# A second attention that forms keys and values per head, multiplies values in pairs of 64 columns, and divides by sums spread through memory

## The chip, the cores and the metric

The kernel runs on one core of one Trainium2 chip, in one launch. The metric is the device time of one execution in microseconds; the time given is the median of several runs. PE is TensorE, DVE is VectorE, ACT is ScalarE, POOL is GpSimd and SP is SyncE, whose queue issues nearly all DMAs. All matmuls of the part that is changed are fp32, and each fp32 matmul shows as two matmul instructions in the profile (a transpose shows as one).

## The reference

Two blocks follow one another on a 1024 x 1024 activation. The first (two layers of latent attention, Fourier mixing and gated merging) isn't touched. The second block projects x, selects keys by an indexer, and runs the attention in which the change lies; an S5 branch, a GLU, an output projection and a layer norm complete it. What the change computes otherwise:

```python
q_lat = einsum('bshd,hcd->bshc', qh, w_uk) * ATT_HEAD_DIM ** -0.5    # 8 heads, d = 64, latent c = 128
_, sel = lax.top_k(index_score, n_sel)                               # 256 of the causal keys per query
s = einsum('bthc,btkc->bthk', q_lat, c_sel)                          # scores against the shared latent
p = softmax(where(valid, s, neg))
o_lat = einsum('bthk,btkc->bthc', p, c_sel)                          # latent output, 128 wide
att = einsum('bshc,hcd->bshd', o_lat, w_uv)                          # back to 64 per head
y = concat([att * silu(gate_a), ssm * silu(gate_s)]) @ w_out         # then layer_norm(ALPHA * x + y)
```

Since the latent c is shared by the heads, `q_lat . c` equals `q . (w_uk c)`, a key of 64 per head, and `(p c) w_uv` equals `p (c w_uv)`, a value of 64 per head. Both orders compute the same function.

## The kernel before

A list of instructions is written out by hand for each engine; semaphores tie them. The eight PSUM banks (128 x 512 fp32 each) have a "full" semaphore that the producer raises and a "free" one that the reader raises; `begin(b)` waits for free, `arrive(b)` for full.

**Ahead of the attention.** DVE picks the top keys by rounds of MAX8 and MATCH_REPLACE8 (L2012, L2013) over `sel`; for the last query tile 16 of the 32 rounds are left over (the list `LATE`) and done inside the attention, one in each of heads 1, 3, 5, 6, 7 of tiles 4 to 6 and in head 7 of tile 3. PE meanwhile computes gates and, last, the queries qT2 (`gates(5, 0)`, L735). Then it turns w_uk (L892) and forms `qlT`, all 8 heads' latent queries, in 16 matmuls of 64 rows and 512 columns (L903), which ACT copies out of PSUM with the scale (L1490). When they are done SP loads the layer-norm gain and bias (L1149, L1150), each spread over 128 partitions, and DVE waits for these and for the GLU (L2046, L2047) before the first unit.

**The attention.** A unit u is one of 8 query tiles t (128 queries) and one of 8 heads h, with the heads inner. Tile t sees t + 1 key tiles. For each unit: PE scores against `c2T` (L918, one or two matmuls of up to 512 columns over 128 rows), into banks 0/1 or 2/3 in turn. DVE adds the mask, takes the maximum and writes to `Pb2` (L2110). ACT exponentiates and sums the row (L1519). PE turns the t + 1 key tiles of the probabilities (L930), DVE copies the first four from PSUM (L2095, `turned`), ACT the rest (L1513). PE issues the scores of unit u + 1 before it turns unit u, so one unit is ahead.

Per tile, four heads' turned probabilities are side by side, and `latent_out` (L940) multiplies each key tile of `c2` by all four at once, 512 columns wide: one call at head 5, one at head 1 of the next tile. ACT copies the result (L1495), `att_out` (L948) multiplies each head's 128 x 128 latent by w_uv, DVE scales by the inverted sums (L2051, L2053), `att_turn` (L956) turns the tile back, and DVE multiplies it into the gate (L2060). `out_half` (L969) is half of an output product, 4 fp32 matmuls of 512 columns; four of them run at heads 4 to 7 for the tile before. DVE adds the residual x (`residual`, L2069), takes the mean (L2076) and centres it (L2078); ACT squares and takes the root (`ln_std`, L1500, L1501; the root's table and the exponential's are loaded in turn); DVE finishes the norm (`layer_norm`, L1842, L2087), and SP writes the tile out and reloads the next x tile (L1090).

The first attention (L535 to L575) already multiplies values as the change will: `v_tok` in pairs of 64 columns, two units side by side in the array.

## Time and profile before

| | us |
|---|---|
| median of 3 runs | 2722.01 (2720.97 to 2722.5) |
| the profiled execution, its own time | 2720.86 |
| its span in the trace | 2719.1 |
| busy: PE / DVE / ACT | 2574.2 / 1364.7 / 796.1 |
| mean granted clock of TensorE | 0.976 |
| first unit of the second attention starts at | 2398.85 |

Times in the trace count from the start of the span. A busy time is the union of an engine's instructions; a matmul's own duration is longer than its distance from the next, because they are pipelined. So "start to start" is what a matmul costs in a row of them, and the chain (which cuts each piece where the next begins) shows it directly.

### The profile page before, as it was taken

The numbers are of one execution on the slowest core, as the hardware profiler recorded it, in microseconds if no ns is written. First come the engines' busy times: TensorE is split into PE (matmuls) and PEld (weight loads), VectorE is DVE, ScalarE is ACT, GpSimd is POOL, SyncE is SP. The second block draws the span as 40 slices with busy tenths as digits, with TensorE's granted clock in tenths as the row PEclk, the third lists the DMA queues.
The fourth block names the chain that finished last, engine by engine and source line by source line (L and its number), as shares of the span: only waits on it lengthen the run. The fifth ranks groups of instructions, "written<-read, shape, count | busy, mean of one in ns | idle before, by whom it ended". The sixth has DMA issues, their size and how long they took to land.

```text
span 2719.1 us, 30167 instructions
## 1 busy us (share of the span) xinstructions
PE 2574.2 (95%) x12253; PEld 1785.7 (66%) x12253; DVE 1364.7 (50%) x2194; ACT 796.1 (29%) x1420; POOL 348.1 (13%) x463
## 2 busy tenths in 40 slices
PE   7998999899999999989979999999989989989997
PEld 6855887776666887578868766667547444445553
DVE  2353777321113243357762211122689999955763
ACT  3332445221112142334451111131352113143341
POOL 0012230000000000133200000000043863100000
PEclk9998999999999999989989999999999999999998
DMA  5010000301113121000002111130301011010000
GB/s 194 28 62 1 1 1 1 88 24 47 47 47 123 34 94 58 31 1 1 1 32 55 47 47 41 33 121 15 118 32 39 2 41 39 31 62 31 31 16 31
DMA packets 106378, 118.89 MB, mean 44 GB/s; under 512 B 20704, under 2 KB 76736, under 8 KB 106240
## 3 DMA queue, kind: packets, MB, share of 16 engines
q1 hardware_dynamic: 105088, 112.76, 13.3%
q10 hardware_dynamic: 1152, 4.19, 0.4%
q8 instruction: 98, 1.61, 0.2%
q14 instruction: 40, 0.33, 0.0%
HBM read 98.92 MB, written 16.84 MB: 43 GB/s over the span
## 4 chain that ended last, share of the span: by engine, by line
PE 84%; DVE 8%; ACT 4%; issue 1%; POOL 1%; SPq 1%; DMA 1%; DVEq 0%; POOLq 0%; ACTq 0%
PE PS L644 8%; PE PS L614 6%; PE PS L617 6%; PE PS L620 6%; PE PS L551 6%; PE PS L441 4%; PE PS L575 4%; PE PS L561 4%; PE PS L969 4%; PE PS L735 4%; PE PS L882 2%; PE PS L658 2%; PE PS L661 2%; PE PS L664 2%; PE PS L940 2%; PE PS L486 2%
## 5 line engine op out<-in xcount | busy, mean ns | idle before, releaser
L614 PE MATMUL PS<-hHi,R2bR 128*128 128x512 f32 x768 | 306.3, 399 | 15.4 <-ACT rows L1323 15.4
L617 PE MATMUL PS<-hLo,R2bR 128*128 128x512 f32 x768 | 300.2, 391 | 0.0
L620 PE MATMUL PS<-hHi,R2bR 128*128 128x512 f32 x768 | 300.0, 391 | 0.0
L1737 DVE TENSOR_TENSOR R2bR<-W,R2bR 128x1024 fp32r<-128x1024 f32 x48 | 57.5, 1222 | 309.6 <-ACT R2bR L1311 309.6
L1343 ACT ACTIVATE R3a<-PS,pT 128x512 f32<-128x512 f32 x64 | 42.3, 687 | 467.5 <-PE PS L620 467.5
L614 PEld LDWEIGHTS PS<-hHi,R2bR 128*128 128x128 f32 x768 | 145.1, 189 | 48.8 <-ACT rows L1323 15.7
L1712 DVE TENSOR_REDUCE negm<-PS 128x1 f32<-128x1024 f32 x128 | 156.5, 1223 | 28.3 <-PE PS L551 23.4
L735 PE MATMUL PS<-hT,W 128*128 128x512 f32 x384 | 166.8, 595 | 0.0
L617 PEld LDWEIGHTS PS<-hLo,R2bR 128*128 128x128 f32 x768 | 145.1, 189 | 33.0 <-issue 3.3
L1295 ACT ACTIVATE R2b<-PS,negm 128x1024 f32<-128x1024 f32 x128 | 142.4, 1112 | 78.6 <-DVE negm L1712 78.6
L620 PEld LDWEIGHTS PS<-hHi,R2bR 128*128 128x128 f32 x768 | 145.0, 189 | 30.4
L2165 POOL TENSOR_TENSOR R<-R,rsh 128x768 f32<-128x768 f32 x16 | 23.8, 1486 | 1028.0 <-DVE rsh L1669 831.8
L561 PE MATMUL PS<-ident,R2b 128*128 128x128 f32 x1024 | 139.0, 279 | 7.3 <-ACT R2b L1295 5.6
L2012 DVE MAX8 ssc<-R2a 128x8 f32<-128x384 f32 (+4 forms) x160 | 132.4, 828 | 5.4
L575 PE MATMUL PS<-R2b,R 128*64 128x128 f32 x2048 | 128.3, 279 | 6.5 <-DVE R2b L1725 3.2
L735 PEld LDWEIGHTS PS<-hT,W 128*128 128x128 f32 x384 | 73.0, 191 | 91.1 <-issue 91.0
L575 PEld LDWEIGHTS PS<-R2b,R 128*64 128x64 f32 x2048 | 112.7, 139 | 29.1 <-issue 22.3
L2013 DVE MATCH_REPLACE8 R2a<-ssc,R2a 128x384 f32<-128x384 f32 (+4 forms) x160 | 129.4, 809 | 0.0
L561 PEld LDWEIGHTS PS<-ident,R2b 128*128 128x128 f32 x1024 | 114.3, 142 | 22.5 <-issue 13.2
L1772 DVE TENSOR_TENSOR R3a<-R3a,PS 128x512 f32<-128x512 f32 x64 | 43.8, 685 | 162.4 <-PE PS L644 162.3
L441 PE MATMUL PS<-W,hT 128*128 128x256 f32 (+1 forms) x512 | 122.3, 399 | 0.7 <-DMA W<-in_w_in 0.5
L969 PE MATMUL PS<-W,R 128*128 128x512 f32 x256 | 117.2, 603 | 0.8 <-DVE R L2060 0.8
(347 smaller groups left out, 4758.5 us busy)
## 6 DMA issues: line engine op xcount, KB each, us to landing
W<-in_w_in SPq DMA_DIRECT2D x10, 2048.0 KB, 8.2
W<-in_w_in SPq DMA_DIRECT2D x33, 512.0 KB, 4.9
xres<-R SPq DMA_DIRECT2D x3, 4096.0 KB, 18.8
W<-in_w_out SPq DMA_DIRECT2D x6, 2048.0 KB, 8.0
R<-xres SPq DMA_DIRECT2D x2, 4096.0 KB, 18.3
W<-in_c_dft_s SPq DMA_DIRECT2D x2, 2052.0 KB, 9.2
R<-in_x ACTq DMA_DIRECT2D x8, 512.0 KB, 7.9
W<-in_w_in SPq DMA_DIRECT2D x4, 1024.0 KB, 6.8
```

Of the source, the lines that this page charges most:

```text
L441: mm = pe.matmul(o[:, 0:hi - lo], hT[:, k, t * P:(t + 1) * P], wc[:, k, lo:hi], start=(k == 0), stop=(k == 7))
L551: mm = pe.matmul(PS[:, b + n, :], x[0:QK, t * P:(t + 1) * P], y[0:QK, n * 512:(n + 1) * 512], start=(i == 0), stop=(i == 2))
L561: mm = pe.transpose(o[:, k * P:(k + 1) * P], Pb[u % 2][:, c * P:(c + 1) * P], ident[:, :])
L575: mm = pe.matmul(PS[e * VD:(e + 1) * VD, 6, at_], v_tok[:, k, h, :], PT[e][:, k * P:(k + 1) * P], start=(k == 0), stop=(k == 7))
L614: mm = pe.matmul(o, wHi[c % 2][:, k, :], hHi[:, k, ns], start=(k == 0), stop=False)
L617: mm = pe.matmul(o, wHi[c % 2][:, k, :], hLo[:, k, ns], start=False, stop=False)
L620: mm = pe.matmul(o, wLo[c % 2][:, k, :], hHi[:, k, ns], start=False, stop=(k == 7))
L644: mm = pe.matmul(o, g[:, k0 + k, :], rhs[:, k, n * 512:(n + 1) * 512], start=(k == 0), stop=(k == 3))
L735: mm = pe.matmul(o, wz[:, k, m * P:(m + 1) * P], xT[:, k, n * 512:(n + 1) * 512], start=(k == 0), stop=(k == 7))
L969: mm = pe.matmul(o, mix[:, k, t * P:(t + 1) * P], wo[:, k, :], start=(k == 0), stop=(k == 7))
L1295: act.activation(Pb[u % 2], PS[:, b:b + 2, :].rearrange("p a c -> p (a c)"), ACT.Exp, bias=negm[:, u:u + 1], accum_out=rsum[:, u:u + 1]).t ...
L1712: dve.tensor_reduce(negm[:, u:u + 1], PS[:, b:b + 2, :].rearrange("p a c -> p (a c)"), AX.X, ALU.max, negate=True).then_inc(s_nm, 1)
```

## The change

`qlT`, `wukT`, `latent_out`, `att_out` and `att_turn` go. Keys per head `kT2` (8 matmuls of c2T by w_uk, 512 columns) and values `v2` (8 matmuls) are formed before the attention. Scores take 64 rows, in the upper or lower half of the array by the head's parity. `pv_pair2` multiplies a pair of heads at a time, each key tile by two 64-column matmuls of 128 columns, right into the transposed layout. The inverted sums no longer scale rows there: SP writes them to memory and reads them back spread over 64 partitions per head, and `att_gate` multiplies by them. `lng`, `lnb` move to the buffer of the block's transposed input. The output halves move: n = 1 at heads 5 and 7 of the next tile, n = 0 at heads 1 and 3 of the one after; layer norm and root move to heads 7 and 6.

```diff
-        wukT = CT.rearrange("p i q c -> p (i q c)").rearrange("p (m c) -> p m c", m=4)
-        wuv = Bb.rearrange("p i q c -> p (i q c)").rearrange("p (h d) -> p h d", h=H)
-        qlT = R0
+        wuv = Bb.rearrange("p i q c -> p (i q c)")
+        kT2 = r0[:, 0:4096].rearrange("p (m s) -> p m s", m=4)
+        v2 = r0[:, 4096:8192].rearrange("p (t c) -> p t c", t=NT)
         xt = [r3b[:, 2048:3072], r3b[:, 3072:4096]]
-        lng, lnb = r3a[:, 0:1024], r3a[:, 1024:2048]
-        att = [r3a[:, 2048:2560], r3a[:, 2560:3072]]
-        olT = [r3a[:, 3072:3584], r3a[:, 3584:4096]]
-        PT2 = [hTf[:, i * 4096:(i + 1) * 4096].rearrange("p (k c) -> p k c", k=NT) for i in range(2)]
+        PT2 = [hTf[:, i * 1024:(i + 1) * 1024] for i in range(4)]
+        lng, lnb = hTf[:, 4096:5120], hTf[:, 5120:6144]
+        att = hTf[:, 6144:6656].rearrange("p (m c) -> p m c", m=4)
+        rbc = [hTf[:, 7168 + 512 * i:7680 + 512 * i].rearrange("p (m c) -> p m c", m=4) for i in range(2)]
+        rsums2 = nc.dram_tensor("rsums2", (NT, 2, H // 2, P), F32, kind="Internal").ap()
...
-            qT_free = [bk.count(b) for b in range(8)]
             pe.wait_ge(s2_wk, 16)
-            o = begin(0)
             for m in range(4):
-                mm = pe.transpose(o[:, m * P:(m + 1) * P], wuk[:, m * P:(m + 1) * P], ident[:, :])
-                if m == 0:
-                    mm.then_inc(w_used[1], 1)
-            mm.then_inc(full[0], 1)
-            for b in range(8):
-                pe.wait_ge(free[b], qT_free[b] + (b == 0))
-            for h in range(H):
                 for n in range(2):
-                    b = (1 + 2 * h + n) % 8
+                    b = 2 * m + n
                     o = begin(b)
-                    r_ = slice(VD * (h % 2), VD * (h % 2) + VD)
-                    pe.matmul(o, wukT[r_, h // 2, :], qT2[r_, h // 2, n * 512:(n + 1) * 512],
+                    pe.matmul(o, wuk[:, m * P:(m + 1) * P], c2T[:, n * 512:(n + 1) * 512],
                               start=True, stop=True).then_inc(full[b], 1)
-            marks["qlat"] = bk.count(0)
+            pe.nop().then_inc(w_used[1], 1)
+            pe.wait_ge(s2_wv, 16)
+            for t in range(NT):
+                o = begin(t)
+                pe.matmul(o, c2T[:, t * P:(t + 1) * P], wuv, start=True, stop=True).then_inc(full[t], 1)
             marks["attention"] = list(bk.n)
 
...
-            pe.wait_ge(s2_wv, 16)
 
+                r_ = slice(VD * (h % 2), VD * (h % 2) + VD)
                 for n in range((w + 511) // 512):
-                    mm = pe.matmul(PS[:, b + n, 0:min(512, w - 512 * n)], qlT[:, h, t * P:(t + 1) * P],
-                                   c2T[:, n * 512:min(w, n * 512 + 512)], start=True, stop=True)
+                    mm = pe.matmul(PS[:, b + n, 0:min(512, w - 512 * n)], qT2[r_, h // 2, t * P:(t + 1) * P],
+                                   kT2[r_, h // 2, n * 512:min(w, n * 512 + 512)], start=True, stop=True)
...
-            def latent_out(t, hg):
-                u = H * t + 4 * hg + 3
-                pe.wait_ge(free[4], pt2[u][0])
-                pe.wait_ge(free[5], pt2[u][1])
-                o = begin(6)
+            def pv_pair2(p):
+
+                t, m = p // 4, p % 4
+                pe.wait_ge(free[4], pt2[2 * p + 1][0])
+                pe.wait_ge(free[5], pt2[2 * p + 1][1])
+                if m == 0:
+                    begin(6)
                 for k in range(t + 1):
-                    mm = pe.matmul(o, c2[:, k, :], PT2[hg][:, k, :], start=(k == 0), stop=(k == t))
-                mm.then_inc(full[6], 1)
-                ol_free[hg] = bk.count(6)
-
-            def att_out(t):
-                o = begin(7)
-                pe.wait_ge(free[6], ol_free[1])
-                for h in range(H):
...
-            def att_turn(t):
-                pe.wait_ge(free[7], bk.count(7))
-                o = begin(6)
-                for k in range(4):
-                    mm = pe.transpose(o[:, k * P:(k + 1) * P], att[t % 2][:, k * P:(k + 1) * P], ident[:, :])
-                mm.then_inc(full[6], 1)
-                turn_free[0] = bk.count(6)
...
-            def out_half(t, n, half):
+                    for e in range(2):
+                        h = 2 * m + e
+                        mm = pe.matmul(PS[VD * e:VD * e + VD, 6, m * P:(m + 1) * P], v2[:, k, h * VD:(h + 1) * VD],
+                                       PT2[(2 * p + e) % 4][:, k * P:(k + 1) * P], start=(k == 0), stop=(k == t))
+                if m == 3:
+                    mm.then_inc(full[6], 1)
+
+            def out_half(t, n, half, b=7):
 
                 if (n, half) == (1, 0):
-                    pe.wait_ge(free[6], turn_free[0])
+                    pe.wait_ge(s2_gate, t + 1)
-                o = begin(6 + n) if half == 0 else PS[:, 6 + n, :]
+                o = begin(b) if half == 0 else PS[:, b, :]
-                    mm.then_inc(full[6 + n], 1)
-
-            pt2, ol_free, turn_free = {}, {}, {}
+                    mm.then_inc(full[b], 1)
...
                     scores2(u + 1)
-
-                if h == 5:
-                    latent_out(t, 0)
-                if t >= 1:
-                    if h == 1:
-                        latent_out(t - 1, 1)
-                    if h == 2:
-                        att_out(t - 1)
-                    if h == 3:
-                        att_turn(t - 1)
-                    if h >= 4:
-                        out_half(t - 1, 1 - (h - 4) // 2, h % 2)
+                if u >= 2 and u % 2 == 0:
+                    pv_pair2(u // 2 - 1)
+                if h in (1, 3) and t >= 2:
+                    out_half(t - 2, 0, h // 2)
+                if h in (5, 7) and t >= 1:
+                    out_half(t - 1, 1, h // 2 - 2)
                 p_turn2(u)
-            latent_out(NT - 1, 1)
-            att_out(NT - 1)
-            att_turn(NT - 1)
-            for i in range(4):
-                out_half(NT - 1, 1 - i // 2, i % 2)
+            pv_pair2(4 * NT - 1)
+            for half in range(2):
+                out_half(NT - 2, 0, half)
+            for half in range(2):
+                out_half(NT - 1, 1, half, 4)
+            for half in range(2):
+                out_half(NT - 1, 0, half, 5)
 
 
...
-            sp.wait_ge(full[0], marks["qlat"])
+            for b in range(8):
+                sp.wait_ge(full[b], marks["attention"][b])
             small(lng, a["ln_g_2"][0].partition_broadcast(P), s2_ln)
             small(lnb, a["ln_b_2"][0].partition_broadcast(P), s2_ln)
             sp.wait_ge(s_xsave, 16 * (L + 1))
+            for t in range(2):
+                small(xt[t], xres[t * P:(t + 1) * P, :], s2_xt[t])
             for t in range(NT):
-                if t >= 2:
-                    sp.wait_ge(s2_od[t % 2], 16 * (t // 2))
-                small(xt[t % 2], xres[t * P:(t + 1) * P, :], s2_xt[t % 2])
+                sp.wait_ge(s2_ri, t + 1)
+                for e in range(2):
+                    sp.dma_start(rsums2[t, e].rearrange("m q -> q m"), rinv[:, H * t + e:H * t + H:2],
+                                 allow_slow_non_contiguous=True).then_inc(s2_rw, 16)
+                sp.wait_ge(s2_rw, 32 * (t + 1))
+                for e in range(2):
+                    small(rbc[t % 2][VD * e:VD * e + VD].rearrange("p m c -> p (m c)"),
+                          rsums2[t, e].rearrange("m q -> (m q)").partition_broadcast(VD), s2_bc)
                 if t >= 1:
                     sp.wait_ge(s2_o, t)
                     small(out[0, (t - 1) * P:t * P, :], xt[(t - 1) % 2], s2_od[(t - 1) % 2])
+                    if t + 1 < NT:
+                        sp.wait_ge(s2_od[(t + 1) % 2], 16 * ((t + 1) // 2))
+                        small(xt[(t + 1) % 2], xres[(t + 1) * P:(t + 2) * P, :], s2_xt[(t + 1) % 2])
...
-            o = arrive(0)
-            act.activation(wukT[:, :, :], o.rearrange("p (m c) -> p m c", m=4), ACT.Copy).then_inc(free[0], 1)
-            for h in range(H):
-                for n in range(2):
-                    b = (1 + 2 * h + n) % 8
-                    o = arrive(b)
-                    act.activation(qlT[:, h, n * 512:(n + 1) * 512], o, ACT.Copy, scale=64.0 ** -0.5
-                                   ).then_inc(free[b], 1)
-
-            def latent_copy(hg):
-                o = arrive(6)
-                act.activation(olT[hg], o, ACT.Copy).then_inc(free[6], 1)
+            for b in range(8):
+                o = arrive(b)
+                act.activation(kT2[:, b // 2, (b % 2) * 512:(b % 2 + 1) * 512], o, ACT.Copy, scale=64.0 ** -0.5
+                               ).then_inc(free[b], 1)
+            for t in range(0, NT, 2):
+                o = arrive(t)
+                act.activation(v2[:, t, :], o, ACT.Copy).then_inc(free[t], 1)
...
-                if t >= 2 and h == 2:
+                if u >= 1:
+                    turned_high(u - 1)
+                if t >= 2 and h == 6:
                     ln_std(t - 2)
...
             bk.n = list(marks["attention"])
+            for t in range(1, NT, 2):
+                dve.wait_ge(full[t], bk.n[t])
+                dve.tensor_copy(v2[:, t, :], PS[:, t, :]).then_inc(free[t], 1)
             dve.wait_ge(s2_glu, 8)
             dve.wait_ge(s2_ln, 32)
 
-            def att_norm(t):
+            def sums_inverted(t):
                 dve.wait_ge(free[2], sums2[t])
-                st.link(dve.reciprocal(rinv[:, H * t:H * t + H], rsum[:, H * t:H * t + H]))
-                o = arrive(7)
-                dve.tensor_tensor(att[t % 2].rearrange("p (h d) -> p h d", h=H), o.rearrange("p (h d) -> p h d", h=H),
-                                  rinv[:, H * t:H * t + H].unsqueeze(2).broadcast_to([P, H, VD]), ALU.mult
-                                  ).then_inc(free[7], 1)
+                dve.reciprocal(rinv[:, H * t:H * t + H], rsum[:, H * t:H * t + H]).then_inc(s2_ri, 1)
 
             def att_gate(t):
                 o = arrive(6)
+                dve.wait_ge(s2_bc, 32 * (t + 1))
+                dve.tensor_tensor(att, o.rearrange("p (m c) -> p m c", m=4), rbc[t % 2], ALU.mult).then_inc(free[6], 1)
+                dve.wait_ge(free[6], bk.count(6))
                 m = mix[:, 0:4, t * P:(t + 1) * P]
-                dve.tensor_tensor(m, m, o.rearrange("p (k c) -> p k c", k=4), ALU.mult).then_inc(free[6], 1)
-
-            def residual(t, n):
+                dve.tensor_tensor(m, m, att, ALU.mult).then_inc(s2_gate, 1)
+
+            def residual(t, n, b=7):
 
                 x = xt[t % 2]
                 if n == 1:
...
                 if n == 1:
+                    half_free[t] = (b, bk.count(b))
...
                     turned(u - 1)
+                if t >= 1:
+                    if h == 0:
+                        sums_inverted(t - 1)
+                    if h == 2:
+                        att_gate(t - 1)
-                if h == 5:
-                    bk.take(6)
                 if t >= 2:
                     if h == 0:
+                        residual(t - 2, 1)
+                    if h == 4:
                         residual(t - 2, 0)
-                    if h == 4:
+                    if h == 7:
                         layer_norm(t - 2)
-                if t >= 1:
-                    if h == 1:
-                        bk.take(6)
-                    if h == 2:
-                        att_norm(t - 1)
-                    if h == 3:
-                        att_gate(t - 1)
-                    if h == 6:
-                        residual(t - 1, 1)
             turned(H * NT - 1)
+            sums_inverted(NT - 1)
+            residual(NT - 2, 1)
             residual(NT - 2, 0)
-            bk.take(6)
-            att_norm(NT - 1)
             att_gate(NT - 1)
             layer_norm(NT - 2)
-            residual(NT - 1, 1)
-            residual(NT - 1, 0)
+            residual(NT - 1, 1, 4)
+            residual(NT - 1, 0, 5)
             layer_norm(NT - 1)
```

## Rows read from the trace of the kernel before

**Rows 1.** The page, part 1: busy time of each engine over the whole execution.
```profile
PE 2574.2 (95%) x12253; PEld 1785.7 (66%) x12253; DVE 1364.7 (50%) x2194; ACT 796.1 (29%) x1420; POOL 348.1 (13%) x463
```

**Rows 2.** Busy time by stretch: us, PE, PEld, DVE, ACT, POOL, PEclk, DMA share, GB/s.
```profile
2500.00:2600.00 100.00, 94.89 (x372) 53.99 (x371) 76.63 (x122) 39.24 (x77) 0.00 (x0) 1.00 0.06 22
```

**Rows 3.** Chain in order of time, late tile: start, us, engine, line, count.
```profile
2657.06 6.87 PE PS L940 x16
2663.92 3.43 PE PS L969 x8
```

**Rows 4.** Timeline: value products, then turns, first attention (start, us).
```profile
325.45 1.97 PE L575 MATMUL PS<-R2b,R 128*64 128x128 f32 x32
327.34 1.09 PE L561 MATMUL PS<-ident,R2b 128*128 128x128 f32 x8
```

**Rows 5.** Timeline, late tile and tail of the second attention.
```profile
2642.20 1.89 PE L948 MATMUL PS<-rt,R3a 128*128 128x64 f32 x16
2643.93 1.05 PE L930 MATMUL PS<-ident,R3b 128*128 128x128 f32 x8
...
2677.53 1.04 PE L930 MATMUL PS<-ident,R3b 128*128 128x128 f32 x8
2692.13 16.52 PE L969 MATMUL PS<-W,R 128*128 128x512 f32 x32 [0.78 <-DVE R L2060]
...
2708.69 0.69 DVE L2069 SCALAR_TENSOR_TENSOR R3b<-R3b,PS 128x512 f32<-128x512 f32 x1 [6.11 <-PE PS L969]
2711.72 1.06 ACT L1500 ACTIVATE R2b<-R3b 128x1024 f32<-128x1024 f32 x1 [21.74 <-DVE R3b L2078]
```

**Rows 6.** Timeline from before the attention to its first unit.
```profile
2384.32 0.60 PE L892 MATMUL PS<-ident,R3b 128*128 128x128 f32 x4
2385.66 7.24 PE L903 MATMUL PS<-R3a,u_mid 64*128 64x512 f32 x32 [0.74 <-ACT u_mid L1485]
2393.31 0.43 SPq L1090 DMA_DIRECT2D R3a<-in_ln_b  x1
2395.27 1.21 DVE L2013 MATCH_REPLACE8 R2b<-ssc,R2b 128x1024 f32<-128x1024 f32 x1
2398.85 0.29 DVE L2110 CUSTOM_DVE_ANT_0 R3b<-PS,R2a 128x128 f32<-128x128 f32 x1 [2.38 <-DMA R3a<-in_ln_b]
```

**Rows 7.** Timeline, first VectorE pass of tiles 1, 2, 4 and 7 (queries).
```profile
2407.90 0.42 DVE L2110 CUSTOM_DVE_ANT_0 R3b<-PS,R2a 128x256 f32<-128x256 f32 x1
2430.42 0.56 DVE L2110 CUSTOM_DVE_ANT_0 R3b<-PS,R2a 128x384 f32<-128x384 f32 x1 [0.22 <-PE PS L918]
2497.86 0.82 DVE L2110 CUSTOM_DVE_ANT_0 R3b<-PS,R2a 128x640 f32<-128x640 f32 x1
2626.95 1.22 DVE L2110 CUSTOM_DVE_ANT_0 R3b<-PS,R2b 128x1024 f32<-128x1024 f32 x1
```

**Rows 8.** Timeline around the 64-row matmuls of an earlier stage (L799).
```profile
2150.40 0.39 PE L799 MATMUL PS<-rtp,R3b 64*128 64x128 f32 x4
2150.72 1.12 PE L735 MATMUL PS<-hT,W 128*128 128x512 f32 x2
...
2254.92 0.49 PE L799 MATMUL PS<-R2b,R3b 64*128 64x128 f32 x4
2255.24 0.39 PE L799 MATMUL PS<-R2a,R3b 64*128 64x128 f32 x4
```

**Rows 9.** DMA issues: out<-in, count, KB each, median us to landing.
```profile
W<-in_w_in SPq DMA_DIRECT2D x1, 32.0 KB, 4.9
rsums<-rows SPq DMA_DIRECT2D x2, 32.0 KB, 1.8
R3a<-rsums SPq DMA_DIRECT2D x16, 256.0 KB, 5.6
```

**Rows 10.** One group from 2398 us on: busy us, mean ns | idle before, releaser.
```profile
L930 PE MATMUL PS<-ident,R3b 128*128 128x128 f32 x288 | 43.9, 279 | 15.0 <-ACT R3b L1519 14.7
```

**Rows 11.** TensorE alone by stretch: us, PE busy, granted clock, DMA share, GB/s.
```profile
2398.00:2403.00 5.00, 3.13 (x12) 0.50 0.44 176
```

More of the change, by code:

```diff
@@ L361, in build @@
         s2_xt = [sem(f"x_tile_loaded{i}") for i in range(2)]
+        s2_ri = sem("second_sums_inverted")
+        s2_rw = sem("second_sums_written")
+        s2_bc = sem("second_sums_spread")
+        s2_gate = sem("attention_gated")
         s2_r = sem("centred_ready")
@@ L1143, in _ @@
             small(wuk.rearrange("p (h d) -> p h d", h=H), a["w_uk_2"][0].rearrange("h c d -> c h d"), s2_wk)
-            small(wuv, a["w_uv_2"][0].rearrange("h c d -> c h d"), s2_wv)
+            small(wuv.rearrange("p (h d) -> p h d", h=H), a["w_uv_2"][0].rearrange("h c d -> c h d"), s2_wv)
             for n in range(2):
@@ L1502, in ln_std, with turned_high @@
                                ).then_inc(s2_sq, 1)
+            bk.n = list(marks["attention"])
+            def turned_high(u):
+                t = u // H
+                if t < 4:
+                    return
+                o = arrive(5)
+                w = (t - 3) * P
+                act.activation(PT2[u % 4][:, 512:512 + w], o[:, 0:w], ACT.Copy).then_inc(free[5], 1)
             for u in range(H * NT):
                 t, h = u // H, u % H
-                if u >= 1:
-                    tp = (u - 1) // H
-                    hp = (u - 1) % H
-                    bk.take(4)
-                    if tp >= 4:
-                        o = arrive(5)
-                        n = tp - 3
-                        act.activation(PT2[hp // 4][:, 4:4 + n, (hp % 4) * P:(hp % 4 + 1) * P],
-                                       o[:, 0:n * P].rearrange("p (k c) -> p k c", k=n), ACT.Copy).then_inc(free[5], 1)
                 b = 2 * (u % 2)
-                bk.take(b)
                 act.wait_ge(s2_nm, u + 1)
@@ L2089, in turned @@
             def turned(u):
-                t, h = u // H, u % H
-                n = min(4, t + 1)
+                t = u // H
+                w = min(4, t + 1) * P
                 o = arrive(4)
@@ L2106, in _ @@
                 if u >= 2:
-                    bp = 2 * (u % 2)
-                    dve.wait_ge(full[4 + (((u - 2) // H) >= 4)], bk.count(4 + (((u - 2) // H) >= 4)))
+                    bp = 4 + ((u - 2) // H >= 4)
+                    dve.wait_ge(full[bp], bk.count(bp))
                 dve.tensor_tensor_reduce(Pb2[u % 2][:, 0:w], PS[:, b:b + 2, :].rearrange("p a c -> p (a c)")[:, 0:w],
```

34 lines of the change are left out of this document (7 added, 27 removed).

## The prediction

> **What bounds the kernel now.** The page first: PE is busy 95% of the execution, DVE 50% [rows 1]. That is a mean over stages, so the stretch of the change is read next, in windows. From 2500 to 2600 us PE is busy 94.9 of 100 us and DVE 76.6 [rows 2]: PE bounds the attention, and DVE stands close behind it where the left-over selection rounds lie. Last, the chain of waits: in a late tile it runs through scores, the latent product (16, 6.87 us) and an output half (8, 3.43 us), PE after PE, 0.43 us per instruction of 512 columns [rows 3]. So PE instructions taken out of tiles 1 to 7 come off the time, until another engine or a latency takes over. I take as the loop the stretch from the first pass of tile 1, 2407.90 us [rows 7], to the end of the last turn, about 2678.4 [rows 5]: 270.5 us.
>
> **Removed from PE in the loop.** latent_out has 36 key tiles, two groups of heads and two instructions each, 144 in all; 2 lie in tile 0 and 16 behind the last turn, so 126 x 0.43 = 54.2 us. att_out is 16 instructions in 1.73 us (2642.20 to 2643.93) [rows 5], 7 times in the loop: 12.1. att_turn is 4 transposes at 0.11, the pace of turns by their row (8 in 1.04 us, the last one's length included) [rows 5]: 7 x 0.45 = 3.2. Of the output halves 26 instead of 28 run in the loop: 6.9 us move to the tail. Sum 76.4 us.
>
> **Added to PE in the loop.** Value pairs: the first attention does 8 key tiles of a pair, 32 instructions, in 1.89 us start to start [rows 4], 0.236 per key tile; that is about half of what the same columns cost one after the other (4 x 128 columns at 0.43 / 4), so the two column halves do run together. There are 144 such steps, 3 in tile 0's share and 8 in the tail: 133 x 0.236 = 31.4 us. Scores keep their columns, and 64 rows cost what 128 do: L903, of 64 rows, shows 32 instructions in 7.24 us only because neighbouring ones lie in opposite halves [rows 6]; here the two matmuls of a unit lie in the same half and nothing stands beside them, so 0.43 each stays. No gain there.
>
> **Changes of shape in the array.** New in each unit: from 128-row turns to 64-row scores, and on to something else. In the S5 stage the first four 64-row instructions take 0.32 us (2254.92 to 2255.24) where a group of four is over in 0.22, and after the last group (2150.40 + 0.22) the next matmul starts 0.10 later [rows 8]. So 0.10 in and 0.10 out, 56 units: 11.2 us; and 0.10 more per pair for the way out of the column halves, 28 pairs: 2.8. Together 14 us. Bounds: nothing, and twice it (28). I take 14, it is the nearest row. The Trainium skill, TensorEngine Tiling, section Key Properties, says that changing the tiling mode, not merely the tile, drains TensorE; if each of the five changes per pair of units cost a whole pipeline's length (0.16 us, an estimate: eight turns 0.11 apart last 1.04 [rows 5], so one outlasts its spacing by 0.16), the term would be about 22 and not 14. Loop so far: -76.4 + 31.4 + 14 = -31 us.
>
> **What is given back in the loop.** The new chain for the sums: reciprocal at head 0, two SP writes in 4-byte pieces, wait, two spreads, and att_gate at head 2 waits for them on DVE. Its price isn't in the trace. The write, from below: the first attention's sums, 32 KB in long pieces, land in 1.8 us; from above: 32 KB in 32-byte pieces, 4.9 [rows 9]. The spread, two of 128 KB: between 1.8 again and 5.6, the median where eight of 256 KB run at once [rows 9]. With four issues of 0.4, the chain is 5 to 12 us. I take 8, nearer to the small transfers. DVE has two units from head 0 to head 2; by the PE work of two units at the paces above (scores and turns of tile t, one value pair, and from tile 2 on one output half of 3.43) that is about 2.5 us in tile 1, 6 in tile 2, 7 in tile 3 and 8 to 11 later. Queued behind att_gate on DVE are the copy and the mask pass of the next units, so ACT and the turns wait; PE has turn, scores and, from tile 2 on, an output half of 3.43 to do meanwhile. In tiles 2 to 7 the rest is hidden. Tile 1 has no such half: 5 us of stall. Tile 1's units are short anyway, bound by the round of scores, mask, exponential and turn. Its PE work falls by 8, but I expect 23 us (six units of 1.3, two of 4.7 with an output half, and the stall) where it took 22.5 [rows 7]: gives back 8.5. If PE stands still for some us its clock falls, as it did after the idle time ahead of the first unit, to 0.50 of full [rows 11]; that is in the 23.
>
> Tiles 4 to 6 took 129.1 us [rows 7]; DVE's work there is the same as before (att_gate twice 512 columns, as att_norm and att_gate were), 77% of the time [rows 2], and would be near 90% of the new one. A round is two passes of 1.2 us [rows 6], and head 7 now has one beside the two passes of the layer norm, as wide. I give 2 us back. The root with its two table loads moves from head 2, where little PE work covered it, to head 6, under the output half of head 7. Turns waited 14.7 us for exponentials in all [rows 10]; 3 us of it goes. Loop: -31 + 8.5 + 2 - 3 = -23.5 us.
>
> **Ahead of the attention.** Keys and values are 32 instructions of 512 columns. They start where w_uk's transposes did, at 2384.3, and take 32 x 0.43 = 13.8 us: to 2398.2, where L903 ended at 2392.9 [rows 3, 6]. SP may load lng and lnb only then, since they now lie where the transposed input was; before, lnb was issued at 2393.31 and DVE began at 2398.85, released by it [rows 6]. So the same 5.5 us run from 2398.7, the first unit starts at 2404.5: +5.6 us. DVE's four new copies (0.69 each, as any pass of 512 columns out of PSUM [rows 5]) are hidden under that; selection ends at 2396.5 [rows 6]. The last w_out half is issued 7 us later and has until tile 1, head 5. If lnb were not waited for, the copies would be the cover that is missing, and the start near 2400.5. Tile 0: latency bound, its 2 latent instructions against three pairs, more of it at the low clock: +0.3.
>
> **The tail.** Before: last turn ends at 2678.4, then latent product, att_out, scaling, turn, gate; the last output products start at 2692.13 [rows 5]: 13.7 us. After: last copy (0.9), value pair (2.1), output half pair of tile 6 (6.9). Its residual, mean and centring (3.0, from 2708.69 to 2711.72 for the last tile) and the gate's two passes (2 x 0.69) stand on DVE in a row before the products of tile 7 may start [rows 5]: 4.8 with handovers. The sums' round lies under this. 14.7 against 13.7: +1, and the same end behind it.
>
> **Sum.** -23.5 + 5.6 + 0.3 + 1 = -16.6. The profiled execution took 2720.86, within 0.05% of the median 2722.01. I predict 2704.
>
> **Rivals.**
> (a) The chain of sums bites in every tile: slower. Its place is DVE's wait in att_gate. Four-byte pieces, 512 per write, may cost far more than pieces of 32 bytes. From tile 2 on DVE's gap plus PE's cover is about 11 to 13 us; above this each us of the chain costs 7 per execution, so from some 15 us on the gain is gone; at 18 it would be 2704 + 7 x 5 = 2739. Against it: 1024 pieces of 32 bytes land in 4.9 [rows 9]. 11%. The Trainium skill, DMA: Bandwidth & Descriptors, asks for at least 512 bytes for line rate and says that shorter pieces make the DMA engine read, modify and write; it gives no price for 4 bytes, and no row here shows one.
> (b) DVE takes over in tiles 3 to 6: its heavy heads 4 to 7 hold two rounds more than PE's share covers, 2 us per tile more than I gave, and tile 1 doesn't shrink: 2704 + 8 = 2712. For it: 77% busy at the slower pace. 17%.
> (c) The shape changes cost nothing beside other handovers, and stalls in tile 1 are less: -14 and a little, 2690. 20%.
> (d) The column halves don't overlap in this loop: 133 x 0.236 more, 2735. The same code runs in the first attention [rows 4]: 2%.
> My forecast as it stands: 50%.
>
> **Numbers.** A difference of 0.2% (5.4 us) is about what a measurement can tell from no change. Faster by more: forecast, (b) nearly all, (c): 84%. Within: the upper edge of (b) and the middle of (a), 6%. Slower: 10%. The range goes from (c) with a little room, 2687, to past (b) and into the low end of (a), 2718.
>
> **What would show it.** First unit at 2404 to 2405, released by lnb. Five changes of shape per pair at 0.1. Value instructions (576) at 0.059 us start to start. DVE idle before att_gate's first pass ended by the spread's DMA: some 5 us in tile 1, under 3 in tiles 2 and 3, none after. PE idle of 4 to 5 us before the output products of tile 7. The forecast is wrong if that wait lasts in every tile, if PE falls below 90% in tiles 4 to 6, or if scores or value products have another pace than the rows say.

## The result, and the profile after

The changed kernel takes **2773.86 us** (median of 4 runs, 2769.59 to 2775.74) against 2721.49 for the kernel before (4 runs, 2718.86 to 2722.5): a ratio of 1.0192, interval [1.0174, 1.0209]. 2704 was forecast. The profiled execution took 2769.59 us, its span is 2767.8: 48.7 more than before.

Page of the changed kernel, parts 1 and 4 (busy time; the chain by engine), to set beside [rows 1]:
```profile
PE 2574.7 (93%) x12521; PEld 1782.7 (64%) x12521; DVE 1369.1 (49%) x2198; ACT 786.7 (28%) x1399; POOL 347.8 (13%) x463
...
PE 80%; DVE 9%; DMA 5%; ACT 2%; SPq 1%; issue 1%; POOL 1%; DVEq 0%; POOLq 0%; ACTq 0%
```
PE's busy sum has not grown, 2574.7 against 2574.2; its share has fallen. So the time is idle time, and work at a lower clock hides in the equal sum. The same part of the span as [rows 2], by windows with the same columns:
```profile
2500.00:2600.00 100.00, 80.21 (x375) 45.01 (x376) 59.24 (x99) 26.14 (x55) 0.00 (x0) 0.85 0.09 27
```
PE 80.2 of 100 us where it had 94.9, DVE 59 where it had 77, the clock 0.85: nobody is the bound. Who waits for whom, from 2340 us on (engine, line, releaser: us in total, times, longest):
```profile
ACT R3b L1509 <- DVE negm L2087: 210.9, 57, 12.7
...
DVE hT L2035 <- DMA hT<-rsums: 53.0, 8, 9.6
PE PS L943 <- DVE hT L2035: 49.3, 7, 9.8
...
PE PS L957 <- DVE R L2038: 8.3, 1, 8.3
```
The gate (L2035) waits for the spread sums for all eight tiles, 6.6 us in the mean; and PE waits behind it, 7 times, at the first value product of a tile (L943). Tile 1 by the timeline (start, us, what, wait before it), DVE, SP and PE together:
```profile
2412.15 0.19 DVE L2030 RECIPROCAL sums<-sums 128x8 f32<-128x8 f32 x1
2412.37 1.05 SPq L1142 DMA_DIRECT2D rsums<-sums  x2
...
2421.45 1.33 SPq L1074 DMA_DIRECT2D hT<-rsums  x2
2426.13 0.69 DVE L2035 TENSOR_TENSOR hT<-PS,hT 128x512 f32<-128x512 f32 x1 [9.60 <-DMA hT<-rsums]
...
2426.97 1.12 PE L943 MATMUL PS<-hT,R 128*64 128x128 f32 x8 [9.75 <-DVE hT L2035]
```
From the reciprocal to the gate 14.0 us pass: 9.1 until SP has its two writes back and issues the spreads, 4.7 for the spreads. The transfers, from 2380 us on (count, KB each, median us to landing), to set beside [rows 9]:
```profile
hT<-rsums SPq DMA_DIRECT2D x16, 128.0 KB, 2.9
...
rsums<-sums SPq DMA_DIRECT2D x16, 2.0 KB, 9.1
```
2 KB take 9.1 us, three times what 128 KB take beside them: 512 pieces of 4 bytes each. In a late tile the chain is no shorter and only the wait is, since PE and DVE have more to do in it:
```profile
2673.34 1.22 DVE L2087 CUSTOM_DVE_ANT_0 R3b<-PS,R2b 128x1024 f32<-128x1024 f32 x1
...
2675.09 0.19 DVE L2030 RECIPROCAL sums<-sums 128x8 f32<-128x8 f32 x1
...
2676.51 0.98 SPq L1142 DMA_DIRECT2D rsums<-sums  x2
...
2686.10 1.09 SPq L1074 DMA_DIRECT2D hT<-rsums  x2
...
2690.41 0.69 DVE L2035 TENSOR_TENSOR hT<-PS,hT 128x512 f32<-128x512 f32 x1 [2.95 <-DMA hT<-rsums]
```
15.3 us from reciprocal to gate; 1.4 of them because SP first writes the last output tile out and issues a load of x (2673.45 and 2676.13, both L1074). For the seven gates of the loop the same two rows are 14.0, 14.5, 14.4, 16.4, 17.3, 16.0 and 15.3 us apart. Last, PE alone by stretch (columns as in [rows 11]), ahead of and behind the stall of tile 1, then around that of tile 2:
```profile
2410.00:2415.00 5.00, 5.00 (x14) 0.50 0.12 4
2415.00:2420.00 5.00, 2.21 (x6) 0.50 0.00 0
2420.00:2425.00 5.00, 0.00 (x0) 0.50 0.21 39
2425.00:2430.00 5.00, 3.03 (x13) 0.50 0.05 16
2430.00:2435.00 5.00, 5.00 (x17) 0.50 0.00 0
2435.00:2440.00 5.00, 5.00 (x11) 0.73 0.00 0
2440.00:2445.00 5.00, 5.00 (x21) 1.00 0.00 0
...
2450.00:2455.00 5.00, 3.74 (x11) 1.00 0.00 0
2455.00:2460.00 5.00, 0.00 (x0) 0.82 0.19 44
2460.00:2465.00 5.00, 3.11 (x16) 0.50 0.04 11
2465.00:2470.00 5.00, 5.00 (x9) 0.66 0.00 0
```
In tile 1 the clock stood at 0.50 (1.2 GHz) ahead of the stall too, from the first unit on, and stayed there until some us into the full work behind it; before, it was 1.00 (2.4 GHz) in these stretches. In tile 2 it falls from 1.00 to 0.50 with PE's idle time and is back only in the full work behind it. The mean clock of tiles 2 to 6, by windows from first pass to first pass, is 0.87, 0.85, 0.89, 0.90 and 0.93; before and in e1 it is 1.00 in each.

**Where the 48.7 us are**, from the first VectorE passes of the tiles ([rows 7] and the same timeline after), with the kernel of experiment e1, whose chain is gone, in the last column:

| stretch | before | after | e1 |
|---|---|---|---|
| to tile 0's first pass | 2398.85 | 2400.35 | 2404.44 |
| tile 0 | 9.05 | 11.19 | 11.18 |
| tile 1 | 22.52 | 30.85 | 21.70 |
| tile 2 | 31.24 | 40.91 | 30.22 |
| tile 3 | 36.20 | 44.75 | 34.01 |
| tile 4 | 39.44 | 46.07 | 35.91 |
| tile 5 | 42.36 | 49.00 | 38.98 |
| tile 6 | 47.29 | 50.22 | 42.55 |
| tile 7 to the end | 92.2 | 94.5 | 85.1 |

Each of tiles 1 to 6 is longer than before, and has 7.7 to 10.7 us more than in e1, where 5 us in tile 1 alone were forecast. (e1 begins 4.1 us later: its keys start at 2383.42 and not 2380.71, and DVE has two memsets there. In the traces of this kernel and of e1 to e5 the keys start between 2380.71 and 2387.21, though nothing ahead of them differs: so much the stages before scatter.)

### The profile page after: what moved, and what is told of

The parts are those of the page before. It is cut to its first block, busy times and chain, and to the rows that moved or that the text cites. A ratio compares the mean times of both kernels' runs of the same rounds, so it can differ in the third digit from the quotient of the medians.

```text
span 2767.8 us, 30720 instructions
## 1 busy us (share of the span) xinstructions
PE 2574.7 (93%) x12521; PEld 1782.7 (64%) x12521; DVE 1369.1 (49%) x2198; ACT 786.7 (28%) x1399; POOL 347.8 (13%) x463
## 4 chain that ended last, share of the span: by engine, by line
PE 80%; DVE 9%; DMA 5%; ACT 2%; SPq 1%; issue 1%; POOL 1%; DVEq 0%; POOLq 0%; ACTq 0%
PE PS L649 8%; PE PS L619 6%; PE PS L622 6%; PE PS L625 6%; PE PS L556 6%; PE PS L446 4%; PE PS L580 4%; PE PS L566 4%; PE PS L740 4%; DMA rsums<-sums 3%; PE PS L957 3%; PE PS L887 2%; PE PS L663 2%; PE PS L666 2%; PE PS L669 2%; PE PS L491 2%
## 5 line engine op out<-in xcount | busy, mean ns | idle before, releaser
L619 PE MATMUL PS<-hHi,R2bR 128*128 128x512 f32 x768 | 306.4, 399 | 15.4 <-ACT rows L1318 15.4
L619 PEld LDWEIGHTS PS<-hHi,R2bR 128*128 128x128 f32 x768 | 145.1, 189 | 48.9 <-ACT rows L1318 15.7
L957 PE MATMUL PS<-W,R 128*128 128x512 f32 x256 | 123.4, 629 | 8.3 <-DVE R L2038 8.3
L566 PEld LDWEIGHTS PS<-ident,R2b 128*128 128x128 f32 x1024 | 113.6, 142 | 22.7 <-issue 13.2
```

The costliest lines, as they stand in the source:

```text
L566: mm = pe.transpose(o[:, k * P:(k + 1) * P], Pb[u % 2][:, c * P:(c + 1) * P], ident[:, :])
L619: mm = pe.matmul(o, wHi[c % 2][:, k, :], hHi[:, k, ns], start=(k == 0), stop=False)
L957: mm = pe.matmul(o, mix[:, k, t * P:(t + 1) * P], wo[:, k, :], start=(k == 0), stop=(k == 7))
```

## Experiments

My theory after the result: the chain of the sums holds bank 6, and through it PE, in every tile, and without it the forecast's other terms give a time below before's. Its rivals: the changes of shape cost far more than 14 us, or DVE and the latencies of a round take the gain.

**e1_no_chain** takes the chain away; it leaves out the division by the sums.
```diff
-                (SP: both writes of rinv, wait, both spreads)
+            for i in range(2):                      # DVE, once
+                dve.memset(rbc[i], 1.0)
...
-                dve.wait_ge(s2_bc, 32 * (t + 1))
```


> The changed kernel without its round of sums through memory (no writes, no spreads; the factor in att_gate is a constant 1, so the division by the sums is left out). Theory A (the round is the whole of the loss): DVE's 53.0 us of waits in att_gate and PE's 49.3 us behind it go, with the slow clock after them; what is left is the forecast on record without tile 1's stall, 2699 us, between 2693 and 2706. Rival B (64-row scores and 64-column value products cost more than the rows said): over 2740. Rival C (DVE's new order of passes bounds tiles 4 to 6): 2715 to 2725, with DVE over 90% busy there.

Measured: 2706.49 us, 0.9947 [0.9932, 0.9963], half a us above the range expected. The chain costs 67 us, more than the whole loss.

**e2_rows128** is e1 with scores of 128 rows, so that turns and scores have one shape; the scores of two heads are mixed, and the result is another one.
```diff
-                r_ = slice(VD * (h % 2), VD * (h % 2) + VD)
+                r_ = slice(0, P)
```


> As e1, and the scores take all 128 rows (both heads of a pair are multiplied at once, so the scores of the heads are mixed and the result is another one; the instructions, their columns and their count stay). It prices the change of shape that the 64-row scores bring. Forecast's term: 0.2 us per unit, so 10 to 13 us less than e1. Rival B: 30 us or more less. Rival D (the change of shape hides under handovers): within 3 us of e1.

Measured: 2684.68, 0.9864 [0.9846, 0.9881], 21.8 us below e1, where 10 to 13 were expected: a miss. So the 64-row form costs 0.34 us for each of 64 units in the mean, where 0.20 was forecast (11.2 us for the 56 of the loop). Early part of both by windows, first e1, then e2 (the second line of each is PE alone):
```profile
2400.00:2450.00 50.00, 44.12 (x151) 21.60 (x151) 18.66 (x66) 10.78 (x38) 0.00 (x0) 0.69 0.09 34
...
2425.00:2430.00 5.00, 5.00 (x16) 0.50 0.00 0
```
```profile
2400.00:2450.00 50.00, 42.34 (x193) 23.86 (x193) 23.60 (x78) 12.19 (x42) 0.00 (x0) 0.86 0.11 41
...
2425.00:2430.00 5.00, 4.92 (x24) 1.00 0.00 0
```
In the short tiles e2 runs at a mean clock of 0.86, e1 at 0.69, and gets 193 matmuls done for 151: part of the price is paid in clock. From first pass to first pass e2 is 1.7 us shorter in tile 0 and 7.2 in tile 1 (14.5 for 21.7, at a mean clock of 0.90 for 0.60), half of the 17.8 us between the two traces. In tiles 2, 3, 4 and 6, where both have a clock of 1.00, it is 1.8, 2.1, 1.3 and 1.7 shorter: 0.21 per unit. Tile 1's clock goes with the rows of the scores in every trace: 0.56 to 0.60 in the nine kernels with 64-row scores, 0.76 to 1.00 in the five with 128 (before, e2, e8, e11, e12); why, no run shows. The late tile shows the price at the full clock. Of the kernel after, scores, value pair and turns (start, us):
```profile
2703.33 1.98 PE L917 MATMUL PS<-R,R3a 64*128 64x512 f32 x4
2705.24 1.97 PE L943 MATMUL PS<-hT,R 128*64 128x128 f32 x32
2707.14 1.09 PE L929 MATMUL PS<-ident,R3b 128*128 128x128 f32 x8
```
Four score instructions hold PE for 1.91 us start to start where their own pace gives 4 x 0.43 = 1.72: 0.19 on the way out, and eight turns before them take 0.97 where the pace gives 0.88: 0.1 in. The way in was sized right, the way out at half; the mean of 0.34 is higher than both together, since it holds tile 1 at its low clock. The value pair takes 1.90, as in the first attention [rows 4].

**e3_ln_late**: DVE waits for lng and lnb only where it first reads them, in the layer norm.
```diff
-            dve.wait_ge(s2_ln, 32)
...
                 dve.wait_ge(s2_sq, t + 1)
+                if t == 0:
+                    dve.wait_ge(s2_ln, 32)
```


> The changed kernel, with DVE's wait for the layer norm's gain and bias moved from ahead of the attention to the first layer norm. My reading (the first unit waits 5.0 us for lnb and nothing else is late): 5 us less than the changed kernel, 2769. Rival: the sums' round of tile 0 waits for SP's queue or for the loads just issued, so that what is won at the start is lost at the first gate: no change, 2774.

Measured: 2765.88 (2758.05 to 2772.91), 1.0165 [1.0137, 1.0193]. 8 us less than the changed kernel, but its times overlap with that one's, so the size isn't clear; the trace has the first pass 15.6 us after the keys' first product, where it was 19.6. The wait that goes is this one, of the changed kernel:
```profile
2400.35 0.29 DVE L2087 CUSTOM_DVE_ANT_0 R3b<-PS,R2a 128x128 f32<-128x128 f32 x1 [5.02 <-DMA hT<-in_ln_b]
```

**e4_32_byte_pieces** keeps the whole round through memory and changes the write alone: one DMA, 128 pieces of 32 bytes, for two DMAs with 1024 pieces of 4 together. The spreads read them in the old order, so the factors are permuted and the division isn't the right one (e10 mends that).
```diff
-                for e in range(2):
-                    sp.dma_start(rsums2[t, e].rearrange("m q -> q m"), rinv[:, H * t + e:H * t + H:2],
+                sp.dma_start(rsums2[t].rearrange("e m q -> (e m q)").rearrange("(q i) -> q i", i=H),
+                             rinv[:, H * t:H * t + H]).then_inc(s2_rw, 16)
```


> The changed kernel, with each tile's inverted sums written in one DMA of 128 pieces of 32 bytes where two DMAs of 512 pieces of 4 bytes were (the same 4 KB; the spread reads them as if they lay in the old order, so the factors are permuted). Theory A1 (the number of pieces makes the write slow): the write lands in about 2 us where it took 9, the round takes 7, DVE waits only in tiles 1 to 3, and the time is 2705 to 2718. Rival A2 (any write and read back of memory costs this much, whatever its pieces): write still 7 us or more, time over 2755.

Measured: 2706.18, 0.9948 [0.9932, 0.9964]: as without a chain. Its transfers and the one wait that is left:
```profile
rsums<-sums SPq DMA_DIRECT2D x8, 4.0 KB, 3.1
```
```profile
DVE hT L2034 <- DMA hT<-rsums: 1.6, 2, 1.0
```
Twice the bytes per DMA in 3.1 us instead of 9.1. Two spreads, SP's wait and DVE's, the same queue and bank: all of it is still there, and 67 us are gone. **So it is the form of the write, its 4-byte pieces in two DMAs, and not the round through memory as such.** The Trainium skill, DMA: Bandwidth & Descriptors, Specifications, gives 512 bytes as the least size for line rate; 32 bytes are far below it too, and here they cost nothing that the end sees (2706.18 us for 2706.49).

**e5_gate_late** leaves the slow write and frees the bank: ACT copies bank 6 at head 1, DVE gates the copy at head 4.
```diff
+            def att_copy(t):                        # ACT, at head 1
+                act.wait_ge(s2_gate, t)
+                o = arrive(6)
+                act.activation(att, o.rearrange(...), ACT.Copy).then_inc(free[6], 1)
...
-                    if h == 2:
+                    if h == 4:
                         att_gate(t - 1)
```


> The changed kernel with its round through memory as slow as it is (14 us), but ACT copies the value products out of bank 6 at head 1, so the bank comes free for the next tile's products, and DVE multiplies by the sums at head 4 and not 2. Theory A (the loss is DVE standing in att_gate with bank 6 and the following units behind it): the round now has four units' time, about 5 us in tile 1, 12 in tile 2 and more later, so of 53 us of waits some 15 stay: 2715 to 2728. Rival (the round costs through SP's queue, or through the DMAs' own traffic, wherever it is waited for): over 2750.

Measured: 2714.89, 0.9981 [0.9971, 0.9991]. The write still lands after 8.9 us, and DVE's wait has shrunk from 53.0 to 10.2:
```profile
DVE hT L2044 <- DMA hT<-rsums: 10.2, 5, 5.2
```
So the slow write costs this much only through what stands behind it: 59 of 67 us come back by a later due time and a free bank, two changes that no run took apart.

**e6_sums_turned** makes the spread on the chip: DVE writes 1/sum of each head 64 times, PE turns that into bank 4, ACT copies it.
```diff
+                dve.reciprocal(rb.rearrange("p (h d) -> p h d", h=H),
+                               rsum[:, H * t:H * t + H].unsqueeze(2).broadcast_to([P, H, VD]))
...
+                for m in range(4):                  # PE, head 1, bank 4
+                    mm = pe.transpose(o[:, m * P:(m + 1) * P], rb[:, m * P:(m + 1) * P], ident[:, :])
```


> The changed kernel, with the round through memory replaced by TensorE: DVE writes each head's inverted sum 64 columns wide (one reciprocal of 512 columns), PE turns that tile in four transposes between two units' turns, ACT copies it out. Theory A (nothing but the round's latency in front of att_gate made the change slow): as without the round, 2706, plus 0.5 us per tile for the turn and what it delays: 2706 to 2713. Rival (the extra use of bank 4 between two units' turns stalls each tile by several us, or DVE's wider reciprocal counts): 2720 or more.

Measured: 2719.65 (10 runs), 0.9995 [0.9986, 1.0005]: a miss by nearly 7 us, on one term.
```profile
2546.57 3.34 DVE L2042 RECIPROCAL hT<-sums 128x512 f32<-128x512 f32 x1
```
I had taken it for a pass like any of 512 columns, 0.69; it takes 3.34, where DVE stands at 88 of 100 us.

**e7_turned_ln_tail** adds to e6 the late wait of e3, and gates tile 7 before the residual's second half.
```diff
             residual(NT - 2, 1)
-            residual(NT - 2, 0)
             att_gate(NT - 1)
+            residual(NT - 2, 0)
```


> As e6, and the wait for lng and lnb stands ahead of the first layer norm, and at the end the gate of the last tile goes ahead of tile 6's residual on DVE. Both are on the path by the changed kernel's trace: 5.0 us of wait at the start, 8.3 us of idle PE before the last output products, of which 4 to 5 were DVE's residual, mean and centring. Expected: 9 to 12 us less than e6, 2695 to 2700. Rival (these waits are covered once the round is gone): within 4 us of e6.

Measured: 2708.19, 0.9957 [0.994, 0.9974], 11.5 us below e6, where 9 to 12 were expected (not the 2695 to 2700, which stood on a faster e6). The start's and the tail's waits are real without the chain too; 6.2 us of the gain lie from tile 7's first pass on (80.7 us for 86.9).

**e8_queries_padded**: e7, and POOL lays the queries out with zeros in the other head's rows, so that scores take 128 rows with the right result.
```diff
-                    mm = pe.matmul(PS[...], qT2[r_, h // 2, t * P:(t + 1) * P], kT2[r_, h // 2, ...])
+                    mm = pe.matmul(PS[...], qz[t % 2][:, h, :], kT2[:, h // 2, ...])
...
+                    pool.tensor_copy(z[r_, e:H:2, :], qT2[r_, :, t * P:(t + 1) * P])
```


> As e7, and the scores take 128 rows again: POOL, idle here, copies each tile's queries per head into a buffer whose other 64 rows are zero, and PE multiplies both heads' keys by it. The result stays the same. If the change of shape costs what the run with mixed heads showed (22 us), 2673 to 2680. Rival (POOL's copies come late or slow DVE down): under 8 us less than e7.

Measured: 2694.9, 0.991 [0.9894, 0.9926], above the 2673 to 2680 expected: a miss. e7 had come out some 10 us later than forecast, and the padding wins 13 us where e2 had won 22, with DVE's reciprocal of 3.34 still in each tile. 5.5 us of the gain lie in tile 1 (19.2 for 24.8, at a mean clock of 0.78 for 0.58).

**e9_score_pairs** instead issues both heads' scores alternately, in opposite row halves.
```diff
+                for n in range((w + 511) // 512):
+                    for e in range(2):
+                        r_ = slice(VD * e, VD * e + VD)
+                        mm = pe.matmul(PS[:, 2 * e + n, ...], qT2[r_, m, ...], kT2[r_, m, ...])
```


> As e7, but both heads' scores of a pair are issued alternately, one in the upper and one in the lower half of the array, as L903 did before; per pair the order is turn, turn, scores of the next pair, output half, value pair. If opposite halves run at the same time, scores cost half: about 41 us less on PE, and half the changes of shape. Given back: without a unit's lead PE waits for the exponential where no output half covers it, in tiles 0 and 1, and DVE bounds tiles 4 to 6 at some 34 us each. Expected 2670 to 2685. Rival (latency per pair shows in every tile): 2700 or more.

Measured: 2748.24, 1.0101 [1.0086, 1.0117], a miss. The overlap is there, eight score instructions in 1.92 us start to start where four took 1.91:
```profile
2686.27 1.99 PE L977 MATMUL PS<-R,R3a 64*128 64x512 f32 x8
2688.19 3.70 PE L958 MATMUL PS<-W,R 128*128 128x512 f32 x8
```
But with both score banks written at once and both turns before the next, nothing is left to hide a round:
```profile
2500.00:2600.00 100.00, 78.45 (x410) 42.71 (x410) 70.00 (x104) 28.02 (x61) 0.00 (x0) 0.88 0.06 22
```
```profile
DVE R3b L2113 <- PE PS L977: 47.7, 18, 7.5
...
PE PS L930 <- ACT R3b L1528: 21.8, 10, 3.0
```
PE at 78 us of 100, DVE at 70, clock 0.88: the picture of the changed kernel again, from other waits. DVE waits for scores, and PE for exponentials.

**e10_exact_32_byte** makes e4's layout right: sums stored query by query, all heads spread, DVE picks its own with a step of 8.
```diff
+        rbc_m = rbc.rearrange("p (q i) -> p i q", i=H)[:, 0:H:2, :]
...
+                    small(rbc[VD * e:VD * e + VD, 0:n], rsums2[t, e:H * P].partition_broadcast(VD), s2_bc)
```


> The changed kernel with the write as 128 pieces of 32 bytes (one DMA, eight heads beside each other) and a spread that reads them back in that order, 4 KB to each partition, twice; DVE picks its heads at a stride of 8 elements. Same result, twice the bytes in the spread. If the number of pieces was the whole cause: within 4 us of the run with permuted factors (2706.2). Rival (DVE's strided reads or the larger spread give it back): 2715 or more.

Measured: 2719.2 (10 runs), 1.0002 [0.9992, 1.0011]: a miss by 9 us or more.
```profile
2425.05 1.07 DVE L2036 TENSOR_TENSOR hT<-PS,hT 128x512 f32<-128x512 f32 x1 [2.17 <-DMA hT<-rsums]
```
The pass with the step takes 1.07 us for 0.69, and the spreads are twice as large (256 KB, 3.6 us): DVE still waits, 6.3 us in 4 tiles, and PE behind it 9.3 us in 6. The mean clock of tiles 3, 4 and 5 is 0.91, 0.88 and 0.96, where e4 has 1.00.

**e11_32_byte_ln_tail_padded** joins e10, the two waits of e7 and the padding of e8.

> As the one before, with the wait for lng and lnb at the first layer norm, the last gate ahead of tile 6's residual, and queries padded with zeros by POOL to 128 rows. From 2706: 8 to 11 less for start and tail, 13 to 20 less for the shape: 2676 to 2687, faster than both kernels. Rival (DVE bounds tiles 4 to 6 once PE has less to do): 2690 or more.

Measured: 2693.82, 0.9901 [0.9886, 0.9917], above the 2676 to 2687 expected; DVE waits 17.8 us in 6 tiles for the spread, where e10 had 6.3 in 4, and PE 13.2 us behind it.

**e12_turned_padded** is e8 with the reciprocal over 8 columns and a copy that repeats it, in place of one over 512.
```diff
-                dve.reciprocal(rb..., rsum[...].unsqueeze(2).broadcast_to([P, H, VD]))
+                st.link(dve.reciprocal(rinv[:, H * t:H * t + H], rsum[:, H * t:H * t + H]))
+                dve.tensor_copy(rb..., rinv[...].unsqueeze(2).broadcast_to([P, H, VD]))
```


> As the run with turned sums, padded queries, late wait and tail (2694.9), but the reciprocal is taken of 8 columns and then spread by a copy of 512, since the trace showed 3.34 us for a reciprocal of 512 columns. DVE wins 2.4 to 2.8 us per tile where it is the one waited for: 2680 to 2688. Rival (that time was covered): within 4 us of 2695.

Measured: **2686.23** (2683.16 to 2688.92), 0.9867 [0.9851, 0.9884]: faster than both kernels, 34 us below before (2719.77 in its runs beside this one) and 88 below the changed one. Its groups (busy us, mean ns | idle before):
```profile
L2046 DVE COPY hT<-sums 128x512 f32<-128x512 f32 x8 | 3.4, 428 | 0.3
...
L2045 DVE RECIPROCAL sums<-sums 128x8 f32<-128x8 f32 x8 | 1.5, 193 | 0.0
```
0.62 us per tile do what took 3.34, and the time falls by 8.7 us against e8.

## Why the prediction was wrong

**The step that failed** is the price of the sums' round: "the chain is 5 to 12 us. I take 8, nearer to the small transfers." It took 14.0 to 17.3 in the seven tiles of the loop, 15.4 in the mean, above the upper end too. That end came from a row of 32-byte pieces [rows 9]; the write's own are of 4 bytes, and it took 9.1 in the median. It wasn't bounded from the far side at all: no row had such pieces, and the range took the nearest for a limit. Rival (a) named this place and got 11%.

**Its second half failed too:** "In tiles 2 to 7 the rest is hidden." Rival (a) put the slack at 11 to 13 us and 7 us per execution on each us above it; by that 15.4 us of chain would cost 17 to 31. It cost 67 (e1). DVE's time up to head 2 had been sized right: the round less the wait leaves 4.4 us in tile 1, 6.9, 7.8, 8.0, 9.3 and 10.0 in tiles 2 to 6 and 12.4 in tile 7, where 2.5, 6, 7 and 8 to 11 were forecast. PE's cover was not there. The forecast had turn, scores and an output half run on while DVE waits, but not which PE instruction needs the gate: the first value pair of a tile takes bank 6, which the gate frees, and in PE's order it comes right behind the scores of head 3, ahead of the turn and the output half. So PE stops with DVE, 49.3 us in 7 waits for DVE's 49.2, and 3.9 more before tile 7's output (8.3, where e1 has 4.4). That leaves about 14 of the 67, and they are work at a lower clock: from tile 1's first pass to the end PE has the same 1284 instructions in both traces, and is busy 283.0 us, in e1 267.3: 15.7 us more for the same work; the clock of tiles 2 to 6 is 0.85 to 0.93 for 1.00. e5 is the proof from the other side: same slow write, bank free and gate later, 59 us back.

**What held.** The start: in the kernel after, the first pass comes 19.6 us after the keys' first product (2380.71), before it was 14.5 after w_uk's transposes [rows 6]: +5.1 for +5.6, released by lnb as written. The time itself, 2400.35 for 2404.5, is off because the keys started 3.6 us earlier than taken, within the scatter of the stages before; that e1's 2404.44 meets 2404.5 is luck, since it is 21.0 behind its keys, with two memsets of 1.03 in all. Value pairs: 1.90 us for 1.89. Removed products: tile 6 of e1 is 4.7 us shorter than before. By the forecast's prices it loses 13.4 (26 latent instructions, att_out, att_turn), gains 6.4 (27 key tiles of a pair) and 2.0 of shapes: 5.0. Tiles 2 to 6 together are 14.9 shorter, by the same prices 17.2.

**The second term that was off** is the price of the 64-row form. Without its chain the kernel is 15 us below before (e1); the forecast without its 5 us of stall gives 22. By tiles the missing 7 are 3.7 in tile 1 (21.7 us in e1 for 18), 1.8 in tile 0 and some 2 in tiles 2 to 6. Tile 1's own parts in the forecast (six units of 1.3, two of 4.7, 5 us of stall) make 22.2 of the 23, which leaves 0.8 for a lower clock; it was 0.60 there. With 128 rows it was 0.90, and tile 1 took 14.5 (e2). The other part is the way out of the 64-row form, 0.19 for 0.10. I had read it behind instructions of 128 columns [rows 8] and taken it for that of 512. At the full clock the rows of e2's section give 0.1 in and 0.19 out for each unit, and at most 0.05 for the way out of the pairs (1.90 us for 1.89, then eight turns in 1.02 for 0.97): 0.63 per pair of units, 18 us in the loop for 14. The Trainium skill, TensorEngine Tiling, Key Properties, has a drain at each change of mode; this trace agrees in that each way costs something, and the 18 lies between my 14 and the 22 that I had worked out with the drain.

**Smaller misses.** Tile 0 costs 2.1 more, forecast 0.3, 1.7 of it gone with 128 rows (e2). The tail: from the last turn's end to the last products 18.1 us (2723.8 to 2741.88) for 13.7, forecast 14.7; 3.8 of it is the gate's wait for the spread. Rival (b), DVE in tiles 3 to 6, did not show: tiles 4 and 5 of e1 are 3.5 and 3.4 shorter than before, at 82 of 100 us for DVE. Its other half, a tile 1 that doesn't shrink, did (21.7 for 22.5 without the chain), by the clock and not by DVE. DVE as the bound shows only where its own work is raised (e6). Rivals (c) and (d) are out by e2 and by the value pairs' 1.90.

**Left open.** Whether the 9.1 us come from the number of pieces, from their size or from there being two DMAs. 1024 pieces of 32 bytes landed in 4.9 in a load [rows 9], and 128 of 32 bytes in 3.1 in a write; no run wrote 1024 of 32 or 128 of 4. Nor which of e5's two changes brings its 59 us, nor why 64-row scores go with a low clock in tile 1.

## What to carry to other kernels

Price a small transfer by its pieces, and where no row has such pieces, say that the upper end is unknown, or take the way that doesn't hang on it (here a repeat on DVE and four transposes; with the padding and the later waits of e12 34 us below before). For each new wait find the buffer that the waiting instruction frees and the next instruction on any engine that needs it: the slack is the work up to there, and PE pays for a stall once more in clock (15.7 us on 52 of idle time here). Compare a price in a stretch where both kernels have the same clock, before it is called the price of an instruction.

## What the runs showed of the hardware

- Two writes of 2 KB each in 4-byte pieces land after 9.1 us (median, 7.9 to 11.5); one of 4 KB in 32-byte pieces after 3.1 (1.4 to 5.0).
- A reciprocal of 512 columns takes 3.34 us on VectorE, of 8 columns 0.19; a copy that repeats 8 columns to 512 takes 0.43.
- A pass of 512 columns out of PSUM with the second operand at a step of 8 elements takes 1.07 us, at a step of 1 0.69.
- 64-row scores of 512 columns between 128-row work cost 0.1 us on the way in and 0.19 on the way out at the full clock; over the attention it is 21.8 us for 64 units (e1 against e2), half of it in tiles 0 and 1. Scores in opposite row halves, issued alternately, run together: 8 in 1.92 us.
- The mean granted clock of tile 1 was 0.56 to 0.60 in nine kernels with 64-row scores and 0.76 to 1.00 in five with 128-row scores. Stalls of 5.6 to 8.5 us in tiles 2 to 6 went with a mean clock of 0.85 to 0.93, where it is 1.00 without them.
